# Two attentions' queries computed with tokens on partitions, and the first stage's casts and squares on other engines

## What is computed

```
def rms_norm(x, g):
    return x * rsqrt(mean(x * x, axis=-1) + EPS) * g

x = x + 0.5 * swiglu_ffn(rms_norm(x, g_ffn1), w_ffn1_in, w_ffn1_out)
h = rms_norm(x, g_mix)
rq, rk, rv, rg, dq, dk, dv, mq, gates = split(h @ w_in)
# differential attention: 8 heads, two 64-wide maps each, causal
dqn = rms_norm(dq.reshape(B, S, 8, 2, 64), g_diff_q)
dkn = rms_norm(dk.reshape(B, S, 8, 2, 64), g_diff_k)
a = softmax(dqn0 @ dkn0.T / 8) - lam * softmax(dqn1 @ dkn1.T / 8);  dif = a @ dv
# memory attention: 4 heads of 256, 256 memory tokens
mo = softmax(rms_norm(mq, g_mem_q) @ rms_norm(mk, g_mem_k).T / 16) @ mv
```

## Time and profile before

| | us |
|---|---|
| median of 3 runs | 2389.83 (2389.46 to 2392.04) |
| the profiled execution | 2388.88 |
| its span, slowest core | 2387.8 (cores 2382.2 to 2387.8) |
| PE busy | 2321.8, 97% of the span |
| DVE, ACT, POOL busy | 1222.9, 984.8, 149.8 |

### The profile page before, as it was taken

The page is one execution under the profiler, slowest core; times in us unless marked ns, Lnnn a source line. Parts: engine busy times, 40 slices in busy tenths (PEclk is TensorE's granted clock), DMA queues, the critical chain, the costliest instruction groups (busy, mean ns, idle before and its releaser), DMA issues.

```text
span 2387.8 us, 34149 instructions; the slowest of 8 cores (2382.2 to 2387.8 us)
## 1 busy us (share of the span) xinstructions
PE 2321.8 (97%) x13284; PEld 1112.4 (47%) x13284; DVE 1222.9 (51%) x2359; ACT 984.8 (41%) x1679; POOL 149.8 (6%) x173
## 2 busy tenths in 40 slices
PE   6999999999999999999999999999999999999998
PEld 2444444444444444454444465555554444444443
DVE  5577334485565552113444576677754655344334
ACT  3111110357767764144631487788851221111110
POOL 1000000230000000000000111121100000000000
PEclk9999999999999999999999999999999999999999
DMA  8221221353442424342102200201305322321313
GB/s 232 49 50 24 52 38 34 82 135 58 67 79 37 83 43 74 54 73 51 20 16 46 46 12 10 45 13 28 48 10 141 71 45 36 53 36 24 47 18 141
DMA packets 86779, 132.69 MB, mean 56 GB/s; under 512 B 71648, under 2 KB 72032, under 8 KB 75360
## 3 DMA queue, kind: packets, MB, share of 16 engines
q0 software_dynamic: 10512, 75.50, 18.8%
q1 hardware_dynamic: 76112, 55.00, 9.1%
HBM read 172.43 MB, written 16.78 MB: 79 GB/s over the span
## 4 chain that ended last, share of the span: by engine, by line
PE 90%; ACT 4%; DVE 2%; POOL 1%; DMA 1%; issue 1%; SPq 0%; POOLq 0%; DVEq 0%; ACTq 0%
PE pw L605 90%; ACT ET L616 2%; POOL acc L628 1%; ACT nrs L616 1%; DMA stg<-w_ffn_in 1%; DMA memT<-mem 0%; ACT L616 0%; DVE dq L620 0%; DVE dU L639 0%; ACT sqf L616 0%; SPq L647 0%; DVE mqn L620 0%; DVE dn L620 0%; ACT nsq L616 0%; ACT sgt L616 0%
## 5 line engine op out<-in xcount | busy, mean ns | idle before, releaser
L605 PE MATMUL pw<-hT,wbuf 128*128 128x512 bf16 x4864 | 1168.5, 381 | 12.3 <-ACT nrs L616 5.6
L605 PEld LDWEIGHTS pw<-hT,wbuf 128*128 128x128 bf16 x4864 | 471.5, 98 | 551.9 <-issue 29.4
L616 ACT ACTIVATE sgf<-pw 128x512 f32<-128x512 f32 x176 | 104.1, 596 | 702.6 <-PE pw L605 702.5
L605 PE MATMUL pw<-uu,wbuf 128*128 128x512 bf16 x1408 | 334.1, 379 | 0.0
L605 PE MATMUL pw<-wbuf,hT 128*128 128x512 bf16 x1280 | 303.2, 379 | 0.2 <-DVE sgR L628 0.2
L616 ACT ACTIVATE ET<-pw 128x1024 bf16<-128x1024 f32 (+1 forms) x288 | 265.9, 975 | 66.9 <-PE pw L605 64.0
L628 DVE TENSOR_TENSOR uu<-pw,sgf 128x512 bf16<-128x512 f32 x176 | 120.8, 690 | 275.7 <-PE pw L605 275.5
L605 PEld LDWEIGHTS pw<-uu,wbuf 128*128 128x128 bf16 x1408 | 137.7, 98 | 166.1 <-issue 0.2
L605 PEld LDWEIGHTS pw<-wbuf,hT 128*128 128x128 bf16 x1280 | 123.0, 98 | 137.5 <-issue 0.6
L605 PE MATMUL pw<-Vd,ET 128*128 128x129 bf16 x2176 | 173.2, 220 | 8.3 <-DVE dU L639 4.5
L620 DVE SCALAR_TENSOR_TENSOR xT<-pw,xT 128x512 f32<-128x512 f32 x192 | 130.4, 688 | 78.4 <-PE pw L605 74.7
(11 more groups left out here) (120 smaller groups left out, 2153.6 us busy)
## 6 DMA issues: line engine op xcount, KB each, us to landing
wbuf<-w_in POOLq DMA_DIRECT2D x26, 1024.0 KB, 8.3
wbuf<-w_ffn_in POOLq DMA_DIRECT2D x21, 1024.0 KB, 10.3
wbuf<-w_ffn_out POOLq DMA_DIRECT2D x10, 1024.0 KB, 9.6
xs<-xT SPq DMA_DIRECT2D x4, 2048.0 KB, 11.6
xT<-x SPq DMA_DIRECT2D x6, 1024.0 KB, 22.9
wbuf<-w_br_ret POOLq DMA_DIRECT2D x4, 1024.0 KB, 8.0
wbuf<-w_mem_kv POOLq DMA_DIRECT2D x4, 1024.0 KB, 10.5
x2l<-xs SPq DMA_DIRECT2D x2, 2048.0 KB, 14.5
```

The source lines that it names most:

```text
L605: return Op("pe", lambda e: e.matmul(out, lhsT=lhsT, rhs=rhs, start=start, stop=stop, **kw), reads, writes, n / 2400.0 + 0.003, 0.17, sign ...
L616: return Op("act", lambda e: e.activation(out=out, in_=in_, func=func, **kw), reads, writes, c, 0.08, fuse=("accum_out" not in kw), tab=TA ...
```

## The change

1. **Memory queries with tokens on partitions.** `m_proj` now holds a block of `hT` (128 tokens) in PE and streams the weights, so a bank has 128 tokens by 512 channels (two heads). The sum of squares is then along the free side: a new `m_q` lets ACT square with an accumulated sum and do Ln and Exp on two numbers per partition, DVE scales, and a flip brings the result back to channels on partitions (`mqn`, 32 flips). The values get a column of ones, so that the product with `EM` held in PE gives the softmax sum beside the output; DVE divides, and a second flip writes `MO` (32 flips). The ones-products are gone from both.
2. **Differential queries and keys likewise.** One bank holds q and k of a head for 2 x 128 tokens; 16 matmuls of 256 columns take the place of 8 of 512. ACT squares, DVE multiplies by the gains and reduces, ACT does Ln and Exp on 8 numbers per partition, POOL scales, a flip writes `dqk` (64 flips). Heads are projected at `i * 3 - 3` pairs, not `i * 4 - 4`.
3. **The first weight casts** go from POOL to ACT, behind the first norm; **the first squares** of tiles 1 to 3 go from DVE to POOL and more to ACT (tile 0 keeps its order).
4. **Constant products in idle time:** `warm` multiplies the constant block into a bank nobody reads, wherever PE has nothing to do by the planner's clock up to 27 us.
5. The planner's table: a flip (any DMA under 1.0 us in its table) is now said to land 3.0 us after its transfer, without queueing behind other DMAs; the load of the memory tokens is said to land 8 us later than before. `nsq` has 4 slots; retention's merge no longer waits for `sgt` and `rcore`.

```diff
+WARM = 27.0
+LAND = 3.0
...
         if op.dma is not None:
-            self.t_dma = max(self.t_dma, s + 0.5) + op.dma
-            fin = self.t_dma + 2.0
+            if op.dma < 1.0:
+                fin = s + op.dma + LAND
+            else:
+                self.t_dma = max(self.t_dma, s + 0.5) + op.dma
+                fin = self.t_dma + 2.0
...
-                    e = (("act", "dve") * 4 if done[0] == "f1" else (...))[k]
+                    e = (("act", "dve") * 4 if done == ("f1", "h", 0) else ("act", "pool", "act", "act", "pool", "act", "pool", "act")
+                         if done[0] == "f1" else (...))[k]
...
         def m_load():
             yield spdma(memT[:, :], mem_d[:, :], [], [memTb], 1 << 20)
+            memTb.w_fin += 8.0
...
+        def m_q(b, mi, c, key):
+            for hh in range(2):
+                yield act(nrs[j][:, 0:256], bk(b)[:, hh * 256:hh * 256 + 256], AF.Square, ..., accum_out=s1)
+            ln = act(s2, s2, AF.Ln, ...)
+            yield act(s2, s2, AF.Exp, ...)
+            for hh in range(2):
+                yield stt(nsq[n][:, sl], bk(b)[:, sl], mss[...], gmq[:, :], ALU.mult, ALU.mult, ...)
+            yield flip(mqn[mi][:, c * TT:(c + 1) * TT]..., nsq[n][:, :], ...)
...
+            for cp_ in range(2):
+                for cc in range(2):
+                    for mt in range(2):
+                        yield mm(bk(b)[:, 0:257], EM[e][:, c * 128:(c + 1) * 128], mv4[:, mt, hm, 0:257], ...)
+                    yield Op("dve", lambda e, b=b, rc=rc: e.reciprocal(out=rc, in_=bk(b)[:, 256:257]), ...)
+                    yield ts(nsq[n][:, sl], bk(b)[:, 0:256], rc, None, ALU.mult, ...)
+                yield flip(MO[:, o * TT:(o + 1) * TT]..., nsq[n][:, :], ...)
...
         def d_qk(b, h, i):
+            yield act(nrs[j][:, :], bk(b), AF.Square, [bkb[b]], [nrsb[j]], TT)
+            yield tt(qraw[r]..., bk(b)..., gqk..., ALU.mult, ...)
+            yield Op("dve", lambda e: e.reduce_sum(out=ss, in_=nrs[j]...), ...)
+            yield act(ss, ss, AF.Ln, ...)
+            yield act(ss, ss, AF.Exp, ...)
+            yield tt(nsq[n]..., qraw[r]..., ss..., ALU.mult, ..., eng="pool")
+            yield flip(sl..., nsq[n][:, :], [nsqb[n]], [dqkb[h % 2][i]], 131072)
...
-            yield lambda: ("rcore", 14) in flags and len(Tm_s.held) == 0 and len(sgt_s.held) == 0
+            yield lambda: len(Tm_s.held) == 0
...
+        def warm():
+            while P.t["pe"] < WARM:
+                yield Op("pe", lambda e: e.matmul(bk(6), lhsT=identb, rhs=cbf[:, :], start=True, stop=True), ...)
...
         def w_cast():
+            yield flag(("f1", "h", 0, 0))
-                yield Op("pool", lambda e, dst=dst, src=src: e.tensor_copy(out=dst, in_=src), ...)
+                yield act(dst, src, AF.Copy, [stgb[k]], [w0b[k]], TT)
```

More of the change, by code:

```diff
@@ L1258, in m_core @@
+        def m_core(t, hm, mi, key):
+            for c in range(4):
+                yield flag((key, c))
+            q4 = mqn[mi][:, :].rearrange("p (c a q) -> p c a q", c=4, a=4)
             es_ = []
             for mt in range(2):
+                yield EM_s.free
+                e = EM_s.get()
+                es_.append(e)
                 yield mk_pool.free
@@ L1270, in m_core @@
                 mk_pool.put(b)
-            mqn_s.put(mi)
-            yield mk_pool.free
-            b = mk_pool.get()
-            for mt in range(2):
-                yield mm(bk(b), ones1, EM[es_[mt]][:, :], mt == 0, mt == 1, [EMb[es_[mt]], b_cbf], [bkb[b]], TT)
-            yield rlm_s.free
-            rlm_s.get()
-            yield act(rlm[:, :], bk(b), AF.Ln, [bkb[b]], [rlmb], TT)
-            mk_pool.put(b)
-            yield act(rlm[:, :], rlm[:, :], AF.Exp, [rlmb], [rlmb], TT, scale=-1.0)
@@ L1333, in d_qk @@
-            d_main.put(m)
-            yield act(nrs[j][:, :], nrs[j][:, :], AF.Exp, [nrsb[j]], [nrsb[j]], TT, scale=-0.5)
-            dst, db, g = (dq[pp], dqb[pp], PV_GDQ) if which == 0 else (dk[pp], dkb[pp], PV_GDK)
-            yield stt(dst[:, t * TT:(t + 1) * TT], qraw[r][:, :], pvec[:, g:g + 1], nrs[j][:, :], ALU.mult, ALU.mult,
-                      [qrawb[r], nrsb[j], b_const], [db[t]], TT)
-            nrs_s.put(j)
-            qraw_s.put(r)
-            flags.add(("dqk", h, t, which))
+            yield qss_s.free
@@ new lines, in d_qk @@
+            u = qss_s.get()
+            ss = qss[:, u * 8:u * 8 + 8]
+            yield Op("dve", lambda e: e.reduce_sum(out=ss, in_=nrs[j][:, :].rearrange("p (g d) -> p g d", g=8),
+                                                   axis=mybir.AxisListType.X), [nrsb[j]], [qssb[u]], 0.7)
+            nrs_s.put(j)
+            yield act(ss, ss, AF.Ln, [qssb[u], b_eps], [qssb[u]], 60, bias=epsc[:, 0:1], scale=1.0 / 64.0)
+            yield act(ss, ss, AF.Exp, [qssb[u]], [qssb[u]], 60, scale=-0.5)
@@ L1342, in d_vev @@
+            nsq_s.put(n)
+            flags.add(("dqk", h, i))
         def d_vev(b, g, c):
@@ L1411, in d_score @@
                     if p == 0:
-                        yield lambda: all(("dqk", h, t, c) in flags for t in range(qt // 2 + 1) for c in range(2))
+                        yield lambda: all(("dqk", h, i) in flags for i in range(qt + 1))
                 ops = []
@@ L1499, in d_tail @@
             yield stt(el, l0, EPS, l0, ALU.mult, ALU.mult, rawb + [drcb[u]], [drcb[u]], 4)
-            yield dn_s.free
-            j = dn_s.get()
+            yield nsq_s.free
+            j = nsq_s.get()
             for i in range(4):
```

253 lines of the change are left out of this document (147 added, 106 removed).

## The result

The changed kernel takes **2447.3 us**, against 2389.8 before: a ratio of 1.023, 95% interval 1.020 to 1.026. The prediction was 2365, with 2347 to 2382 as its range, and slower at 5%. It was wrong in sign. In some executions the cores of one die run at a lower granted clock throughout; times and ratios leave these out, but the ratios of e8 and e10 still hold executions, about 20 us longer, in which one pair of cores did so, and without them e8 took 2382 to 2384 us and e10 2371 to 2375 (0.993).

A forecast was written before the change was run, and what follows sets the result against it. The prediction took PE to bound the kernel, busy 2321.8 of 2387.8 us. Start -7.5, tokens -4, memory attention -10, differential attention -11 and retention +8 gave -24.5, so 2365 us, range 2347 to 2382.

The forecast's parts named there:

- Retention: Retention, changes of head: PE waits for key flips and `rets` buffers beside weight loads; +8 us, bounds 0 and +20.
- key flips: Retention: second state update moves ahead of the second key flip's landing beside a load; PE waits 2.5 us.
- Late flips everywhere: Rival, all stages: flips land late beside loads; retention +18, memory -7.5, differential -9; 2382 us, chance 0.17.
- Flips one after another: Rival, memory attention: a flip starts only when the one before has landed; +62, about 2427 us, chance 0.04.
- Differential attention: Differential attention: -13.3 us of PE work, late flips before first scores cost 1 to 4; -11, bounds -14 and -6.
- Memory attention: Memory attention: -13.5 us of PE work, less 3.5 us of new waits; -10, bounds -14 and -4.
- (b): Memory attention: SP 83% taken by 64 flips, queued flips push the last back 1 to 2 us; 3.5 with (c).
- (c): Memory attention's start: first flips meet two weight loads, PE waits 2 to 5 us; 3.5 with (b).
- Start: First FFN block: ends near 58 us, not 65.6, as squares and norms run under tile 1's products; -7.5, bounds -3 and -10.
- Memory tokens: Memory tokens' squares: PE's 3.15 us wait goes, as the planner puts that product 7 us later; -4, bounds -3 and -5.

The follow-up runs named there:

- e8: e1 plus a third buffer for the memory attention's flipped queries (`mqn`): 1.0019 of the kernel before, 2382 to 2384 us without disturbed executions.
- e10: e1 plus three own buffers for memory outputs, leaving the four shared ones to query flips: 0.9966 of the kernel before, 2371 to 2375 us without disturbed executions.
- e2: The kernel before with only the planner's new figure for small DMAs, no added flips: 1.0196 of the kernel before.
- e9: The changed kernel, figure and TensorE order kept, with a third `rets` buffer lent to retention: 1.0045 of the kernel before, 2398 us.
- e13: The changed kernel, order kept, with nine weight loads of retention's heads 1 to 3 fetching 64 of 4096 columns: 1.0042 of the kernel before, 2398 us.
- e14: e10 with the two memory merge weight loads held back until the eighth query flip has landed: 0.9940 of the kernel before.
- e5: The kernel before with only the differential attention's part and the fourth shared buffer, old planner figure: 0.9953 of the kernel before.
- e15: e14 with the weight load ahead of the differential attention's first eight flips also held back: 0.9979 of the kernel before.
- e3: The changed kernel with the planner's old figure, without the constant products and the moved casts and squares: 0.9960 of the kernel before.
- e17: e10, order kept, with the two weight loads at the memory attention's start fetching 64 of 4096 columns: 0.9920 of the kernel before, near 2370 us.
- e1: The changed kernel with the planner's old rule, by which a flip queues behind the DMAs before it: 0.9973 of the kernel before.
- e11: e1 without the constant products: 0.9956 of the kernel before, 2380 us.
- e6: The kernel before with the differential attention's part, the start's part and the memory tokens' later due time, old figure: 0.9928 of the kernel before, 2373 us.

## Why the prediction was wrong

**Retention: +8 forecast, bound +20, measured +45.** This is the step that failed. Its mechanism was named: key flips and `rets` buffers beside loads, at three changes of head. Its size was wrong in three ways. I took the longest landing of the earlier trace rows, 10.7 us, as the most that a flip can take. It was the most of one tile on one core: other cores had up to 12.2, and the differential outputs in the same trace up to 18.0. A flip given out beside loads lands when they do, so its landing depends on where it stands among them; the new order puts it between two loads, and it lands after up to 17.7. I let it cost TensorE a part of that, by way of the bank that VectorE should free; but VectorE's whole queue stands, the next rotations in it, and TensorE gets nearly all of it: 12 us each on the slowest core, 9 to 10 on cores 2 and 0, not 6 or 7. And I did not charge the clock: its mean is 0.86 in the two stretches, a mixture of the level of 2.4 and that of 1.2 GHz, and 0.96 over the stage, whose busy time is 10 us longer for the same work. The part that I had priced first, the key flips, took only 4.0. e2, e9 and e13 each show the size by itself.

**Late flips everywhere** was the rival nearest in mechanism to what came; it had +18 at this place, from the same rows.

**Flips one after another**, the rival of the slower side, has the right direction and nearly the time (2427) by a mechanism that isn't there: e14's first seven query flips went out 1.3 to 1.8 us apart and landed after 2.4 us by the median, 4.1 at most. Its nearness is luck.

**Differential attention: -11 forecast; -11 measured (e5).** Right in sum, in part by luck, since two misses cancel. By stages it is -18.4 in the attention and +7.1 before its first scores, where I had 1 to 4: more projections stand ahead of them, TensorE waits 4.7 us once, and the clock is 0.94. I had blamed the load there; e15 shows that it is not the cause. In after as it stands this part won only 9 on the mean core, and on core 4 nothing is left of it, by the wait of 9.83 us shown above: `nsq` buffers, which the new flips now share with the outputs, were no term of mine.

**Memory attention: -10 forecast; about +3 measured (e3).** The work went as forecast, 11 us of 13.5, in a lower clock (0.93). The failed term is "3.5 for (b) and (c)": new waits took 14 us. (c), flips beside the two loads of the earlier trace rows, is 4 us by e17. What e17 leaves, 8 us, is larger, and of it I can say only that it is not those two loads. I counted SyncE's share (83%) but not the buffers: a query flip holds a shared buffer until it has landed, 2.4 to 11.4 us (core 5 of e3), and outputs and queries share four. Parting them is worth 3.9 us of the stage (e10). The slow clock of the stage (0.93) I did not charge either.

**Start: -7.5 forecast; -4 to -5 measured** (538.9 to 534.0; e5, without the start's part, has 538.0). Inside its bounds. Squares of tiles 2 and 3 do run under tile 1's products, but there is a pause that I had not seen, before the block's last sixty or so, and the block ends near 62 on this core, not at 58; core 3 of after:

```profile
8.67 5.28 PE L1661 MATMUL pw<-cbf_sb 128*128 128x512 bf16 x12 [8.67 <-DMA cbf_sb<-cbf]
...
49.14 15.05 PE L617 MATMUL pw<-hT,wbuf 128*128 128x512 bf16 x69 [2.15 <-ACT sgf L628]
```

The constants land at 8.67 here; on the eight cores the first product starts from 6.2 to 9.1, and before from 5.7 to 8.9, so my 6.2 was the early end. Twelve constant products at the slow clock then stand ahead of the first ones-products, as the planner's 3 us also promised this small load too early. In e1 one constant product stands there. That the constant products fill idle time was right; that it is worth anything was not (e11).

**Memory tokens: -4 forecast, -3.4 measured** (555.6 to 552.2 in e3, 555.5 in e5 without it; -2 in e1 and e6).

The sum with what the stages of after measured: start -5, retention with the tokens +45, memory attention and its merge +6.5, differential attention -9, rest +1: +39 on the mean core. The other 19 of the 57.5 are the slowest core's: about half in retention, where the same three waits are longest (13.0 at most, 10.6 on core 0), and the rest in the differential attention. In after the memory merge took 122.2 us, in e1 113.5; the output flips under the 3 us figure are a likely reason, as e9 and e13 have it too (122.6 and 122.8), but that was not tried by itself, and e2, with the figure and without these flips, does not have it (112.4).

The Trainium skill ("DMA: Bandwidth & Descriptors", Queues, rings and completion order) has each DMA engine go round its queues packet by packet, by which I had put a flip beside a load at about 5 us. The trace does not agree: 8.8 to 17.7 us, the flip landing after the load.

## What to carry to other kernels

A number in a planner's model is an edit to every stage that it plans; look first at the stage that has no idle time and leans on it. Where a small transfer goes out beside large ones, take the end of the large ones as its landing, and not the longest landing seen so far. Where an engine works in order, price a late transfer at the whole queue behind the instruction that waits for its buffer, and see whether one more buffer takes the wait away before moving work. Add the clock that a wait of 10 us costs to the wait itself.

## What the runs showed of the hardware

- A flip of 128x512 lands in 2.4 us by itself. Beside 1 MB loads most land within 2 us after a load has: retention's outputs after up to 17.7 us (16.3 in the case shown), a differential output of the kernel before after 18.0, and one `dqk` flip of after (core 4, 1676.7 us) after 21.8. SyncE's queue was held for 9.0 us by one such flip (e14), for 1.19 by the median.
- With two loads cut from 1 MB to 16 KB, the query flips given out from 1087 to 1112 us landed in 4.3 us at most, in place of 11.2 (core 3 of e17 and of e10). The whole stage won 4 us by it.
- A TensorE pause of 11 to 13 us brought the mean granted clock of its 50 us down to 0.86 (600 to 650 and 700 to 750 us, core 4 of after).
- Eight cores that run the same program without exchange lay 35 us apart in after, and 6 us apart before and in e6.
